# A routed block on one core: the second modulation inside the joining stage's tile loop, the expert table by one-hot products

## The reference, cut to what matters

```python
merged = (sigmoid(g_fox + b_gate[:D]) * (out_fox @ w_proj_fox)
          + sigmoid(g_dsa + b_gate[D:]) * (out_dsa @ w_proj_dsa))
x = x + gt1 * (merged @ w_out)
h2 = rmsnorm(x, norm2_g) * (1.0 + sc2) + sh2
g_logits = h2 @ w_grp + b_grp            # 4 groups
e_logits = h2 @ w_exp + b_exp            # 32 experts, 8 in a group
# best group, then the two best experts in it; softmax weights of both
order = argsort(expert)                  # rows sorted by expert
y = (silu(xs @ w1[e]) * (xs @ w3[e])) @ w2[e]     # a ragged product over 32 experts
# block two starts from a modulation that depends on c_2 alone:
mod = silu(c_2) @ w_ada_2 + b_ada_2      # 1024 x 6144 weights, 24 MB
```

## Time and profile before

| | |
|---|---|
| median of 3 runs | 3974.26 us (3968.25 to 3984.0) |
| the profiled execution | 3977.95 us, its span 3976.1 us |
| PE busy | 3738.9 us, 94% of the span |
| DVE busy | 1672.6 us, 42% |
| ACT busy | 960.3 us, 24% |
| POOL busy | 453.6 us, 11% |
| moved by DMA | 533.31 MB, mean 134 GB/s |
| span of `joining`, up to the experts' first product | 996 to 1356 us |

### The profile page before, as it was taken

The page is one execution under the profiler, slowest core; times in us unless marked ns, Lnnn a source line. Parts: engine busy times, 40 slices in busy tenths (PEclk is TensorE's granted clock), DMA queues, the critical chain, the costliest instruction groups (busy, mean ns, idle before and its releaser), DMA issues. The chain is left out here.

```text
span 3976.1 us, 46083 instructions
## 1 busy us (share of the span) xinstructions
PE 3738.9 (94%) x18228; PEld 1979.1 (50%) x18228; DVE 1672.6 (42%) x2790; ACT 960.3 (24%) x1993; POOL 453.6 (11%) x334
## 2 busy tenths in 40 slices
PE   6999999999898699999977999999898999999999
PEld 3554444555454344444434457876655444444443
DVE  2479998655322100000012334555453333343246
ACT  2311111554232122121214312222243311111001
POOL 0032231311210210101011111211000000000000
PEclk8979999999999699999996899999899999999999
DMA  4213232021424898989857222222113111111434
GB/s 172 74 38 118 76 140 85 24 62 35 131 100 169 292 339 329 341 329 343 329 214 255 92 70 94 94 81 86 53 35 117 40 43 43 43 43 43 129 111 156
DMA packets 301194, 533.31 MB, mean 134 GB/s; under 512 B 31220, under 2 KB 110244, under 8 KB 298702
## 3 DMA queue, kind: packets, MB, share of 16 engines
q1 hardware_dynamic: 279118, 472.27, 34.5%
q0 software_dynamic: 12592, 43.66, 2.8%
q10 hardware_dynamic: 9296, 14.75, 1.0%
HBM read 462.77 MB, written 67.85 MB: 133 GB/s over the span
## 5 line engine op out<-in xcount | busy, mean ns | idle before, releaser
L561 PE MATMUL ch_side<-aT,space 128*128 128x512 f32 x896 | 392.1, 596 | 0.0
L1684 DVE TENSOR_SCALAR ex_y<-ex_y,ex_entry 128x1024 f32<-128x1024 f32 x32 | 41.1, 1284 | 635.0 <-PE ex_y L1604 635.0
L561 PEld LDWEIGHTS ch_side<-aT,space 128*128 128x128 f32 x896 | 168.6, 190 | 213.7 <-issue 210.9
L2908 PE MATMUL en_bank<-en_h,en_up 128*128 128x512 f32 x528 | 233.8, 592 | 0.0
L1588 PE MATMUL ex_a<-ex_w,ex_xT 128*128 128x512 f32 x512 | 227.7, 598 | 6.2 <-ACT ex_xT L1655 6.2
L1604 PE MATMUL ex_y<-ex_w,ex_actT 128*128 128x512 f32 x512 | 225.1, 592 | 0.7 <-ACT ex_actT L1667 0.7
L1588 PE MATMUL ex_b<-ex_w,ex_xT 128*128 128x512 f32 x512 | 225.0, 592 | 0.0
L2070 PE MATMUL mx_duo<-mx_chunks,mx_region 128*128 128x512 f32 x384 | 181.6, 628 | 0.0
L667 DVE MAX8 ch_best<-ch_score 128x8 f32<-128x384 f32 (+5 forms) x192 | 171.6, 894 | 6.1
L668 DVE MATCH_REPLACE8 ch_score<-ch_best,ch_score 128x384 f32<-128x384 f32 (+5 forms) x192 | 168.0, 875 | 0.0
L2908 PEld LDWEIGHTS en_bank<-en_h,en_up 128*128 128x128 f32 x528 | 100.2, 190 | 125.8 <-issue 125.8
(11 more groups left out here) (522 smaller groups left out, 5908.2 us busy)
## 6 DMA issues: line engine op xcount, KB each, us to landing
ex_w<-exp_w SPq DMA_DIRECT2D x96, 2048.0 KB, 13.5
en_up<-w_down SPq DMA_DIRECT2D x132, 256.0 KB, 3.7
mx_x<-proj_padded SPq DMA_DIRECT2D x96, 256.0 KB, 3.6
space<-ada_w SPq DMA_DIRECT2D x8, 2048.0 KB, 14.2
space<-w_ada SPq DMA_DIRECT2D x8, 2048.0 KB, 19.8
aT<-w_in SPq DMA_DIRECT2D x7, 2048.0 KB, 8.6
...
```

The costliest lines, as they stand in the source:

```text
L561: last = nc.tensor.matmul(side_ps[i % 2][:, 0:width], hT[:, k, t * P:(t + 1) * P], by[:, k, 0:width], start=k == 0, stop=k == KD - 1)
L1684: nc.vector.tensor_scalar(y[b][:, :], y_ps[:, :], entry[b][:, 2:3].bitcast(F32), None, ALU.mult).then_inc(y_ready, 1)
L2908: last = nc.tensor.matmul(to[:, :], a[:, k, :], b[:, k, :], start=k == 0, stop=k == HK - 1)
```

## The change

It has four parts.

1. The second modulation moves into the tile loop and from PE to DVE. `weigh` sums a 128x8x512 chunk times the vector over the 8 slices k, one TENSOR_SCALAR and seven SCALAR_TENSOR_TENSOR, and leaves 128 partial sums a column; PE adds these up in `row_columns` with a column of ones, ahead of a tile's logits. Even tiles take one chunk ("first", between `mix(t, 0)` and `mix(t, 1)`), odd tiles two ("second", between `residual(t-1, 0)` and `residual(t-1, 1)`): 12 in all. There is one buffer of 2 MB for the weights, so chunk n + 1 is issued when chunk n is weighed.
2. The last two tiles' steps on PE stand in another order, and the routing runs in two batches, tiles 0 to 5 before the last residual, tiles 6 and 7 behind their logits. Counts and block numbers are made with fewer instructions.
3. The table no longer goes through DRAM. POOL compares 16 row numbers with an iota (32 TENSOR_SCALARs of 128x128), DVE compares block numbers with another, and 16 products of PE give an SBUF table of codes, 16 more one of weights. The fill of the DRAM table, 16 indirect DMAs and the load are gone.
4. The first expert's weights are loaded by SP at the end of the tile loop, into SBUF that `joining` has finished with, and the first two gathers are issued in `joining`. The experts' weight and row buffers lie in `joining`'s space.

```diff
@@ joining, SP
-            load_mod(0)
-            for t in range(2, NT):
-                sp.wait_ge(mixed, 2 * (t - 1))
-                load_gate(t)
-                sp.wait_ge(scaled, t - 1)
-                sp.wait_ge(x_stored[t % 2], 16 * (t // 2))
-                load_x(t)
+            def load_mod(n):
+                if n >= 1:
+                    sp.wait_ge(weighed, KD * n)
+                sp.dma_start(w_mod, ...[:, :, n * CH:(n + 1) * CH]).then_inc(mod_loaded, 16)
+
+            load_mod(0)
+            for t in range(NT):
+                if t >= 2:
+                    sp.wait_ge(scaled, t - 1)
+                    sp.wait_ge(x_stored[t % 2], 16 * (t // 2))
+                    load_x(t)
+                load_mod(chunk_at["first", t] + 1)
+                if t + 2 < NT:
+                    sp.wait_ge(mixed, 2 * (t + 1))
+                    load_gate(t + 2)
+                if ("second", t) in chunk_at and t + 1 < NT:
+                    load_mod(chunk_at["second", t] + 1)
             sp.wait_ge(product, 2 * NT)
-            load_mod(1)
-            load_mod(2)
+            sp.dma_start(w2[0], ...exp_w2...).then_inc(g.w2_loaded[0], 16)
             sp.wait_ge(mixed, 2 * NT)
-            load_mod(3)
-            sp.wait_ge(projected, 2 * NT)
-            load_mod(4)
-            load_mod(5)
-            for n in range(BUFS, CHUNKS):
-                sp.wait_ge(mod_summed, n - BUFS + 1)
-                load_mod(n)
+            sp.dma_start(w13[0][0], ...exp_w1...).then_inc(g.w1_loaded[0], 16)
+            sp.wait_ge(weighed, KD * CHUNKS)
+            sp.dma_start(w13[0][1], ...exp_w3...).then_inc(g.w3_loaded[0], 16)
@@ joining, PE
+                for n in turns[t + 2]:
+                    pe.wait_ge(weighed, KD * (n + 1))
+                    row_columns(nc, logit_bank(t)[:, 64 + 4 * n:68 + 4 * n], acc[n % ACCS], ones[:, 0:1])
                 for k in range(KD):
-                    last = nc.tensor.matmul(bank[5][:, 0:R], hT[t % 2][:, k, :], w[:, k, :], ...)
+                    last = nc.tensor.matmul(logit_bank(t)[:, 0:R], hT[t % 2][:, k, :], w[:, k, :], ...)
...
+            project(NT - 1, 0)
+            flip_x(NT - 2)
+            project(NT - 1, 1)
+            logit(NT - 2)
+            flip_x(NT - 1)
+            count(0, bank[0][:, 0:EARLY * NE], slice(0, EARLY)).then_inc(counted, 1)
+            logit(NT - 1)
+            count(1, bank[1][:, 0:(NT - EARLY) * NE], slice(EARLY, NT))
+            nc.tensor.matmul(bank[1][:, 2 * NE:3 * NE], ones[:, :], ahead[:, NT, :], ...).then_inc(counted, 1)
+            pe.wait_ge(owned, 1)
+            nc.tensor.matmul(bank[2][0:1, 0:64], owner[:, 0:1], g.ident[:, 0:64], ...).then_inc(owners, 1)
+            pe.wait_ge(picked, 2 * 2 * NT)
+            for i in range(2 * NT):
+                if i % NT == 0:
+                    pe.wait_ge(placed, i // NT + 1)
+                last = nc.tensor.matmul(bank[3][:, 0:TABLE], picks[1][:, i, :], in_block[0][:, i, :], ...)
+            last.then_inc(told, 1)
+            pe.wait_ge(weighted, 1)
+            for i in range(2 * NT):
+                last = nc.tensor.matmul(bank[4][:, 0:TABLE], picks[0][:, i, :], in_block[1][:, i, :], ...)
+            last.then_inc(valued, 1)
@@ joining, POOL
+            for n, tiles in enumerate((range(EARLY), range(EARLY, NT))):
+                pool.wait_ge(sorted_, n + 1)
+                for t in tiles:
+                    for j in range(2):
+                        at = row_at[:, t, j:j + 1]
+                        nc.gpsimd.tensor_scalar(picks[1][:, 2 * t + j, :], rows_iota, at, code[:, t, j:j + 1], is_equal, mult).then_inc(picked, 1)
+                        nc.gpsimd.tensor_scalar(picks[0][:, 2 * t + j, :], rows_iota, at, None, is_equal).then_inc(picked, 1)
+            pool.wait_ge(tabled, 1)
+            for b in range(2):
+                pool.indirect_dma_start(expert_rows(dsa)[b], None, g.d["xn2"], ...).then_inc(g.gathered[b], 16)
@@ joining, DVE
+            def weigh(at, t):
+                if (at, t) in chunk_at:
+                    n = chunk_at[at, t]
+                    dve.wait_ge(mod_loaded, 16 * (n + 1))
+                    if n >= ACCS:
+                        dve.wait_ge(l_taken, ...)
+                    to = acc[n % ACCS][:, :]
+                    TS(to, w_mod[:, 0, :], g.cT[:, KD:KD + 1], None, ALU.mult).then_inc(weighed, 1)
+                    for k in range(1, KD):
+                        dve.wait_ge(weighed, KD * n + k)
+                        V.scalar_tensor_tensor(to, w_mod[:, k, :], g.cT[:, KD + k:KD + k + 1], to, ALU.mult, ALU.add).then_inc(weighed, 1)
...
+            for t in range(NT):
                 if t >= 2:
                     scale_rows(t - 2)
+                mix(t, 0)
+                weigh("first", t)
+                mix(t, 1)
+                if t >= 2:
+                    take(t - 2)
+                if t >= 1:
                     residual(t - 1, 0)
+                    weigh("second", t)
                     residual(t - 1, 1)
+            scale_rows(NT - 2)
+            route(early)
+            residual(NT - 1, 0)
+            residual(NT - 1, 1)
+            scale_rows(NT - 1)
+            take(NT - 2)
+            sort(early, 0, bank[0][:, 0:EARLY * NE])
+            take(NT - 1)
+            route(late)
...
@@ experts
-            load_up(expert_of(slice(0, 1)), 0)
             load_up(expert_of(slice(1, 2)), 1)
-            load_down(expert_of(slice(0, 1)), 0)
...
-            gather(0, 0)
-            gather(1, 1)
```

More of the change, by code:

```diff
@@ L1270, in _ @@
-            nc.tensor.matmul(bank[1][:, 0:NT * NE], ones[:, :], v, start=True, stop=True).then_inc(counted, 1)
-            for n in range(EARLY, CHUNKS + 1):
-                modulate(n)
+            project(NT - 1, 0)
[6 more added lines that the diff above has]
+            count(1, bank[1][:, 0:(NT - EARLY) * NE], slice(EARLY, NT))
@@ new lines, in sort @@
+            def sort(tiles, n, ranks):
+                many = tiles.stop - tiles.start
+                dve.wait_ge(counted, n + 1)
+                by_choice = ranks.rearrange("p (t e) -> p t e", e=NE).unsqueeze(2).broadcast_to([P, many, 2, NE])
+                chain(TT(both[:, tiles, :, :], o[:, tiles, :, :], by_choice, ALU.mult))
+                chain(V.tensor_reduce(rank[:, tiles, :], both[:, tiles, :, :], AX, ALU.add))
+                chain(TS(turn_i[:, tiles, :], rank[:, tiles, :], 1.0 / P, -0.49609375, ALU.mult, ALU.add))
+                chain(V.tensor_copy(turn[:, tiles, :], turn_i[:, tiles, :]))
+                V.scalar_tensor_tensor(row_at[:, tiles, :], turn[:, tiles, :], -float(P), rank[:, tiles, :], ALU.mult, ALU.add).then_inc(sorted_, 1)
@@ L1410, in _, with take @@
+            chain(V.memset(ahead[:, 0, :], 0.0))
+            def take(t):
+                dve.wait_ge(logits, t + 1)
+                for n in turns[t + 2]:
+                    at = slice(6 * D // P + 4 * n, 6 * D // P + 4 * n + 4)
+                    TT(g.modT[:, at], logit_bank(t)[:, 64 + 4 * n:68 + 4 * n], g.biasT[:, at], ALU.add)
+                TT(L[:, t, :], logit_bank(t)[:, 0:R], bias[:, :], ALU.add).then_inc(l_taken, 1)
+            for t in range(NT):
                 if t >= 2:
                     scale_rows(t - 2)
-                if t < NT:
-                    mix(t, 0)
-                    mix(t, 1)
+                mix(t, 0)
+                weigh("first", t)
+                mix(t, 1)
@@ new lines, in _ @@
+            chain(TT(start[:, :], end[:, :], nblk[:, :], ALU.subtract))
+            sort(late, 1, bank[1][:, 0:2 * NE])
+            chain(TT(both[:, :, :, :], o[:, :, :, :], start[:, :].unsqueeze(1).unsqueeze(1).broadcast_to([P, NT, 2, NE]), ALU.mult))
+            chain(V.tensor_reduce(block_at[:, :, :], both[:, :, :, :], AX, ALU.add))
+            chain(TT(block_at[:, :, :], block_at[:, :, :], turn[:, :, :], ALU.add))
+            pairs = lambda a, half: a[:, half * NT // 2:(half + 1) * NT // 2, :].rearrange("p t j -> p (t j)").unsqueeze(2).broadcast_to([P, NT, TABLE])
```

311 lines of the change are left out of this document (147 added, 164 removed).

## The result

The changed kernel takes 3970.10 us (median of 20 runs, 3957.49 to 3977.49) beside 3977.01 for the kernel before: ratio 0.9979, 95% interval 0.9971 to 0.9986. It is 7 us faster, not 28.5. 3970.10 lies outside the range of 3927 to 3966, and what I gave 0.32, a change within half a per cent, is what came. The profiled execution, 3977.49 us, was the slowest of its 20, so its span of 3975.5 us has to be compared stage by stage, not as a whole.

What follows compares the result with a forecast made beforehand. PE, without idle time in the tile loop, and the tail up to the experts' first product were taken as the bound. 8.8 + 7.2 + 1.1 - 45.6 = -28.5 us, from the median 3974.26 to 3946; range 3927 to 3966.

Steps and rivals of the forecast that it cites:

- 10 x 0.88 = +8.8 us, on the path: Tile loop: ten chunks' columns at 0.88 us each lengthen PE's path by 8.8 us, as PE has no slack.
- Rival C: Tail: PE keeps 2.4 GHz there, or in part of it, giving 3939 us; chance 0.10.
- The tail's term: From the end of `project(6, 1)` to the experts' first product: 67.3 us instead of 112.9, so -45.6.
- rival B: Tail: POOL at 0.7 us a comparison holds DVE, products slow; 78 us instead of 67, total 3957; chance 0.17.
- The start: `flip_m(0)` waits behind chunk 0's load and `weigh`: 1032.1 instead of 1024.89, +7.2 us; bounds +6.6 and +17.2.
- rival A: Tile loop: the single weight buffer does not keep up; mild 3950 to 3968, chance 0.14; severe, slower than before, 0.04.
- D's other cause for the start: Start: costs 17 us as the chunk lands late for another reason than the table's fill; 3956; chance 0.10.
- `bias_gate` on POOL: Tile loop: POOL's sum near `mix(t, 0)` pushes DVE by up to 2.5 us, within 6.4 us of slack.
- `told` and `valued`: Tail: two groups of 16 products on PE, each 7.3 us at the slow clock.
- The late routing: Tail, on DVE: 20 operations taking 4.9 us, with 2.5 us added for waiting on POOL.
- the experts' loop is left as it is: Experts' stage: PE does the same products there, so the sum counts no change.
- the signs I had named for being wrong: Tail over 80 us, `weigh` taking 8 us or more a chunk, or the experts' loop changing its pace.

Runs made afterwards that it cites:

- Coded first: The changed kernel with POOL making the 16 comparisons `told` needs ahead of the 16 only `valued` needs; 3956.51 us, ratio 0.9946.
- columns in merge: The changed kernel with the columns' products moved from directly ahead of the logits to the middle of `merge(t, 0)`; 3962.87 us, ratio 0.9961.

## Why the prediction was wrong, step by step

**The step that failed** is "10 x 0.88 = +8.8 us, on the path": the columns' own time was right, and the two runs around it (217.7 without them, 226.7 with them in the merge) measure 9.0. The same products ahead of the logits cost 20.7 us, because they make a thin stretch of 2.6 to 6.4 us out of one of 1.9, and the granted clock halves behind it in 37 of 42 cases. I read a clock of 1.00 from one row of the unchanged loop and took it for a property of the loop; it was one of its mix of products. Rival C asked whether PE would keep its clock in the tail; that the loop could lose it was in none of my cases, and it was the largest miss within joining, 10.8 us.

The Trainium skill, page "TensorE: Matmul & The Clock Gate", section "HAM oscillation — how this bites in real kernels", tells of the clock falling where PE idles between its products. By that rule the loop would have kept it. The measurement decides: PE shows as busy in 34.00 of 34.00 us, and the clock fell.

**The tail's term** was mis-sized on POOL: 0.4 us a comparison by the nearest row, 0.86 and 0.60 measured. That was rival B's price, at which it gave a tail of 78; it came to 72.9, since `told` was late by 8 us, and from its end to that of `valued` it took 11.9 us where my sum had 13.8. Coded first, with a tail 1.6 us under my sum, shows that the rest was right in total. Not in each term: I had 1.8 us for the exponentials with a table load, and ACT had loaded that table at 1295.64 (1.28 us), off the path, so that the two exponentials took 0.23 and 0.19 us.

**Right:**
- The start, +7.2 against +7.6, by the mechanism given. A chunk's `weigh` took 0.49 + 5.48 = 6.0 us (predicted 6.1), and the load for it 8.3 us at the median (8.8 for the first, issued at 1016.7 and used at 1025.49).
- PE waits for nothing in tiles 3, 5 and 7: rival A did not happen. DVE waited 2.20 us for weights in tile 1, and PE 0.21, not 1.1. D's other cause for the start did not arise.
- `bias_gate` on POOL does stretch DVE's sum, within the slack: seven of the sixteen take 2.2 to 4.7 us instead of 0.69. The slack was smaller than I had it, and the push larger. I counted `mix(t, 1)` as three times 0.69, but before the change its sum, at 1196.60, took 2.12 us beside POOL, which leaves 5.0 us of slack and not 6.4; and the longest push was 4.1 us (4.74 less 0.69, in tile 2), not 2.5. With the 0.4 by which `weigh` overruns its slot that is 4.5 of 5.0: that no wait came of it was in part luck.
- `told` and `valued` take 7.06 and 7.07 us, predicted 7.3, with a granted clock of 0.53 from 1292 to 1345, so rival C did not happen. The late routing takes 5.7, predicted 4.9 with 2.5 of waiting.

DVE's rows at the start, and the load group of the modulation weights:

```profile
1025.49 0.49 DVE L1417 TENSOR_SCALAR jn_acc<-space,cT 128x512 f32<-128x512 f32 x1 [4.57 <-DMA space<-w_ada]
1026.01 5.48 DVE L1420 SCALAR_TENSOR_TENSOR jn_acc<-space,cT,jn_acc 128x512 f32<-128x512 f32 x7
```

```profile
DMA to landing us min/median/max: 7.9/8.3/9.5
```

These answer to the earlier trace rows: issued one at a time, the loads land as the row of 8.0 us had it, and not as the median of 19.5.

**What stood outside the sum:** "the experts' loop is left as it is" is true of the code and not of the time, and a change of its pace was one of the signs I had named for being wrong. Its 3.7 us, and 4 to 6.5 us behind it, took most of what the two profiles show as won in joining. From profile to profile the account closes: the change was to be worth 28.5 us and shows 0.5; 16.8 us are missing in joining, 10.2 behind it and 0.9 ahead of it. From median to median it is worth 6.9, which would fit a typical execution that pays less behind joining than the one profiled; no profile shows such an execution of the changed kernel.

**What stays open:** the time behind joining, above; what makes the clock fall behind one thin stretch and not behind another; and the medians, which lie up to 12 us from the profiled execution (columns in merge 3962.87 beside 3953.70, coded first 3956.51 beside 3968.24), since one profile is one draw of the clock. The stage times of `start`, `loop` and `tail` explain where joining's time goes; what a version is worth is read from its ratio.
